# Moving a scratch write and refilling the router stage of a three-layer transformer kernel

## The reference

```python
for l in range(2):                       # hybrid_layer
    proj = x @ w_in[l]                   # gated delta rule (4 heads) + causal attention (8 heads)
    x = layer_norm(ALPHA * x + mix, ...)
    hid = causal_dwconv(x @ w_up, ffn_conv_w) + ffn_conv_b      # 2 x 2816 columns
    x = layer_norm(ALPHA * x + (silu(gate) * val) @ w_down, ...)
# second block
h = rms_norm(x, norm1_g)
# differential attention (4 heads) and dilated attention (8 heads), both with a bias by distance
x = x + concat([oa, od]) @ w_out
h = rms_norm(x, norm2_g)
aff = softmax(h @ w_router)              # 256 tokens x 16 experts
g, idx = top_k(aff.T, 32)                # each expert takes its 32 best tokens
ye = (silu(xe @ wg) * (xe @ wu)) @ wd * g   # xe = h[idx], 16 experts of 1024 x 2816
x = x + scatter_add(idx, ye)
out = rms_norm(x, norm_f_g)
```

## Time and profile before

| | us |
|---|---|
| median of 3 runs | 2328.2 |
| lowest and highest | 2315.79, 2331.55 |
| the profiled execution | 2328.16 |
| its span, first to last instruction | 2326.4 |

### The profile page before, as it was taken

The page is one execution under the profiler, slowest core; times in us unless marked ns, Lnnn a source line. Parts: engine busy times, 40 slices in busy tenths (PEclk is TensorE's granted clock), DMA queues, the critical chain, the costliest instruction groups (busy, mean ns, idle before and its releaser), DMA issues.

```text
span 2326.4 us, 29082 instructions
## 1 busy us (share of the span) xinstructions
PE 1814.8 (78%) x12246; PEld 975.5 (42%) x12246; DVE 469.3 (20%) x1096; ACT 307.6 (13%) x726; POOL 28.8 (1%) x38
## 2 busy tenths in 40 slices
PE   7899999999999999987666666655675666566565
PEld 6675886577488747642212212211221221122122
DVE  2334331253432213530101010100101010010011
ACT  2232221032311102420000000000000000000001
POOL 0010000001010000000000000000000000000000
PEclk9899999999999999987777777777767767676777
DMA  7543443432364346359999999999999999999998
GB/s 244 97 139 127 145 152 128 153 127 98 109 190 145 130 161 247 132 213 403 406 426 423 421 425 425 425 424 426 424 415 425 425 419 424 425 424 424 425 425 334
DMA packets 146422, 693.78 MB, mean 298 GB/s; under 512 B 12732, under 2 KB 62460, under 8 KB 92978
## 3 DMA queue, kind: packets, MB, share of 16 engines
q1 hardware_dynamic: 143346, 683.68, 73.2%
q0 software_dynamic: 2864, 9.00, 2.0%
q10 hardware_dynamic: 144, 0.13, 0.0%
HBM read 688.57 MB, written 4.19 MB: 298 GB/s over the span
## 4 chain that ended last, share of the span: by engine, by line
PE 49%; DMA 40%; SPq 4%; DVE 3%; issue 2%; DVEq 1%; ACT 1%; ACTq 0%
DMA arena<-in_w_up 30%; PE bank L565 16%; DMA arena<-in_w_down 9%; PE bank L588 6%; PE bank L691 6%; PE bank L1097 5%; PE bank L1114 3%; SPq L399 2%; SPq L407 1%; PE bank L890 1%; PE bank L686 1%; PE bank L976 1%; PE bank L914 1%; PE bank L972 1%; DVE arena L1853 1%
## 5 line engine op out<-in xcount | busy, mean ns | idle before, releaser
L1097 PE MATMUL bank<-arena 128*32 128x512 f32 (+1 forms) x3072 | 502.9, 811 | 311.1 <-DMA arena<-in_w_up 293.6
L1097 PEld LDWEIGHTS bank<-arena 128*32 128x32 f32 x3072 | 113.6, 144 | 696.7 <-DMA arena<-in_w_up 418.6
L565 PE MATMUL bank<-arena 128*128 128x256 f32 (+1 forms) x2208 | 383.1, 335 | 7.4 <-ACT arena L1142 3.4
L565 PEld LDWEIGHTS bank<-arena 128*128 128x128 f32 x2208 | 346.1, 192 | 46.4 <-ACT arena L1142 4.6
L1114 PE MATMUL bank<-arena 128*32 128x256 f32 x2816 | 237.5, 484 | 95.0 <-DMA arena<-in_w_down 94.9
L1853 DVE TENSOR_TENSOR arena<-arena,bank 64x256 f32<-64x256 f32 x96 | 40.1, 418 | 772.0 <-ACT arena L1376 770.3
L1114 PEld LDWEIGHTS bank<-arena 128*32 128x32 f32 x2816 | 94.9, 132 | 215.4 <-DMA arena<-in_w_down 132.7
L588 PE MATMUL bank<-arena 128*128 128x512 f32 x352 | 152.0, 591 | 0.0
L691 PE MATMUL bank<-arena 128*128 128x256 f32 x576 | 145.6, 401 | 0.0
L1376 ACT ACTIVATE arena<-bank 64x512 f32<-64x512 f32 (+1 forms) x48 | 23.2, 549 | 823.7 <-PE bank L1097 823.7
L691 PEld LDWEIGHTS bank<-arena 128*128 128x128 f32 x576 | 109.7, 198 | 20.8 <-issue 4.6
(11 more groups left out here) (277 smaller groups left out, 1166.2 us busy)
## 6 DMA issues: line engine op xcount, KB each, us to landing
arena<-in_w_gate SPq DMA_DIRECT2D x128, 1408.0 KB, 19.3
arena<-in_w_up SPq DMA_DIRECT2D x128, 1408.0 KB, 22.3
arena<-in_w_down SPq DMA_DIRECT2D x144, 1024.0 KB, 9.3
arena<-in_w_down SPq DMA_DIRECT2D x32, 1536.0 KB, 12.0
arena<-in_w_up SPq DMA_DIRECT2D x44, 1024.0 KB, 7.0
arena<-in_w_in SPq DMA_DIRECT2D x40, 1024.0 KB, 7.4
arena<-in_w_out SPq DMA_DIRECT2D x12, 1024.0 KB, 7.0
arena<-in_w_down SPq DMA_DIRECT2D x12, 512.0 KB, 3.3
```

The costliest lines, as they stand in the source:

```text
L565: last = mm(ps[bank][:, j * S + lo:j * S + lo + n], w[:, k, c:c + P], xT[:, k, lo:lo + n], start=(k == 0), stop=(k == KT - 1))
L1097: last = mm(ps[b][32 * q:32 * q + 32, 0:n], expert_x[:, k, :], weights[:, q // 2, c:c + n], start=(k == 0), stop=(k == KT - 1))
```

## The change

- The write of the bias rows is split into 12 writes, one a head, and goes behind layer 0's query rotation on GpSimd's queue; each waits for one more of layer 0's up products, from the fourth on. The read back waits for all twelve.
- SyncE: of the three down chunks ahead of gate_up(0, 2), two go behind it and its wait.
- PE: the first tile's logits move behind the second tile's rows; six of their eight k stand before the second tile's transposes, two behind. VectorE takes the first tile's `router_bias` between the second tile's copy of the transposes and its norm.
- PE: products of the identity with columns of `xT` into PSUM bank 0, whose result nobody reads (`keep_clock`): one of 512 columns behind the logits, four behind the transposes of the affinities, one of 256 columns behind each of the two later transposes.
- VectorE: the mask `taken` is signalled when it is made and is transposed by PE on its own, while the scan runs; the scan's numbers are transposed unmasked, and the multiplication by the mask is made on the transposed columns, in the place of the subtraction (the constants `slot` are 1 to 32 now, and 0 stands for "not taken").
- VectorE: the copy into `chosen_pair` comes behind the one-hot rows, with a semaphore of its own; the one-hot of each tile is signalled by itself, and PE begins with tile 0 at once.

```diff
@@ -101,7 +101,7 @@
     parts["causal"] = neg(jj <= i + P)
     parts["tok_row"] = np.broadcast_to(np.arange(S)[None, :], (P, S))
     parts["tok_col"] = np.concatenate([i, i + P], 1)
-    parts["slot"] = np.broadcast_to((np.arange(P) % CAP)[None, :], (P, P))
+    parts["slot"] = np.broadcast_to((np.arange(P) % CAP)[None, :] + 1, (P, P))
     at, cols = {}, 0
     for name, a in parts.items():
         at[name] = (cols, a.shape[1])
@@ -297,6 +297,7 @@
         lambda_parts = Region(second_attention.at + P + 256, after_experts_ring).take(8)
         router, rmax, rsum = second_tiny(T, NE + 1), second_tiny(T), second_tiny(T)
         slots, chosen_pair, places = second_tiny(T, NE + 1), second_tiny(T, 2), second_tiny(2)
+        taken_columns = second_tiny(T, NE)
         topv = second_tiny(8)[0:NE, :]
         routing = xT.rearrange("p x y -> p (x y)")[0:NE, 1280:2048].rearrange("p (x y) -> p x y", y=S)
         affT, affW, taken = (routing[:, i, :] for i in range(3))
@@ -419,10 +420,11 @@
             sp.wait_ge(sem("attended"), at(DEPTH, "attended", 8))
             gate_up(0, 1, 1)
             gate_up(0, 3, 3)
-            for k in range(3):
-                down(0, k)
+            down(0, 0)
             sp.wait_ge(sem("rows_used"), (DEPTH + 1) * ROW_UNITS + 2)
             gate_up(0, 2, 2)
+            for k in range(1, 3):
+                down(0, k)
 
             def stream_gate_up(e, ks):
                 for k in ks:
@@ -461,9 +463,6 @@
             pool.dma_start(const[:, 2 * P + 4:NC], a["consts"][:, 2 * P + 4:NC]).then_inc(sem("const_in"), 16)
 
 
-            pool.wait_ge(sem("bias_copied"), 1)
-            pool.wait_ge(sem("key_products"), 2)
-            pool.dma_start(scratch.rearrange("h (p n) -> h p n", p=P), distance_bias[0:BIAS_HEADS, :].unsqueeze(1).broadcast_to([BIAS_HEADS, P, 2 * S])).then_inc(sem("bias_out"), 16)
             for l in range(DEPTH):
 
                 pool.wait_ge(sem("q_shuffled"), at(l, "q_shuffled", 1))
@@ -472,11 +471,16 @@
                 nc.gpsimd.tensor_tensor(att_q, att_q, table("cos").unsqueeze(1).broadcast_to([P, 4, S]), ALU.mult)
                 pool.drain()
                 nc.gpsimd.tensor_tensor(att_q, att_q, q_swapped, ALU.add).then_inc(sem("q_rotated"), 1)
+                if l == 0:
+                    pool.wait_ge(sem("bias_copied"), 1)
+                    for h in range(BIAS_HEADS):
+                        pool.wait_ge(sem("up_product"), 4 + h)
+                        pool.dma_start(scratch[h:h + 1, :].rearrange("o (p n) -> o p n", p=P), distance_bias[h:h + 1, :].unsqueeze(1).broadcast_to([1, P, 2 * S])).then_inc(sem("bias_out"), 16)
 
 
             pool.wait_ge(sem("rows_used"), DEPTH * ROW_UNITS + 1)
             pool.dma_start(gain, a["norm1_g_2"].broadcast_to([P, D])).then_inc(sem("gain_in1"), 16)
-            pool.wait_ge(sem("bias_out"), 16)
+            pool.wait_ge(sem("bias_out"), 16 * BIAS_HEADS)
 
             def bias_of(h):
                 return scratch[h:h + 1, P - 1:P - 1 + P * (2 * S - 1)].rearrange("o (p n) -> (o p) n", p=P)[:, 0:3 * P]
@@ -1023,12 +1027,19 @@
                         last = tr(ps[H2_BANKS[2 * t + kh]][:, k * P:(k + 1) * P], x[:, t, (4 * kh + k) * P:(4 * kh + k + 1) * P], ident)
                     last.then_inc(sem("h2_transposed"), 1)
 
-            def logits(t):
-
-                pe.wait_ge(sem("h2_copied"), 2 * t + 2)
-                for k in range(KT):
+            def logits(t, ks):
+
+                if ks[0] == 0:
+                    pe.wait_ge(sem("h2_copied"), 2 * t + 2)
+                for k in ks:
                     last = mm(ps[2 + t][:, 0:NE], xT[:, k, t * P:(t + 1) * P], router_w[:, k, :], start=(k == 0), stop=(k == KT - 1))
-                last.then_inc(sem("logits"), 1)
+                if ks[-1] == KT - 1:
+                    last.then_inc(sem("logits"), 1)
+
+            def keep_clock(n, blocks=4):
+
+                for _ in range(n):
+                    mm(ps[0][:, 0:blocks * P], ident, xT[:, 0:blocks, 0:P], start=True, stop=True)
 
             unit_in(L, 7)
             for t in range(T):
@@ -1037,29 +1048,39 @@
                         pe.wait_ge(sem("attended_read"), at(L, "attended_read", k + 1))
                     elif k == 1:
                         rows_transposed(0)
-                    elif k == 3:
-                        logits(0)
                     for nh in range(2):
                         last = mm(ps[ROWS_BANKS[2 * t + nh]][:, :], mixT[:, 4 + k, t * P:(t + 1) * P], slot(7, 1024)[:, k, nh * 512:(nh + 1) * 512], start=(k == 0), stop=(k == 3))
                 last.then_inc(sem("rows_used" if t else "rows_t0"), 2 if t else 1)
+            logits(0, range(6))
             rows_transposed(1)
-            logits(1)
+            logits(0, range(6, KT))
+            logits(1, range(KT))
+            keep_clock(1)
             for t in range(T):
                 pe.wait_ge(sem("affinities"), t + 1)
                 tr(ps[6 + t][0:NE, t * P:(t + 1) * P], router[:, t, 0:NE], ident).then_inc(sem("affinities_transposed"), 1)
-
-            pe.wait_ge(sem("chosen"), 1)
-            for t in range(T):
-                last = tr(ps[7][:, NE * t:NE * t + NE], affW[:, t * P:(t + 1) * P], ident[0:NE, 0:NE])
-            last.then_inc(sem("slots_transposed"), 1)
+            keep_clock(4)
+
+            def token_columns(tokens, ready, bank, done):
+
+                pe.wait_ge(sem(ready), 1)
+                for t in range(T):
+                    last = tr(ps[bank][:, NE * t:NE * t + NE], tokens[:, t * P:(t + 1) * P], ident[0:NE, 0:NE])
+                last.then_inc(sem(done), 1)
+
+            token_columns(taken, "chosen", 5, "taken_transposed")
+            keep_clock(1, 2)
+            token_columns(affW, "counted", 7, "slots_transposed")
+            keep_clock(1, 2)
 
             def rows_gathered(done):
 
-                pe.wait_ge(sem("one_hot"), done)
                 for t in range(T):
+                    pe.wait_ge(sem("one_hot"), T * done - T + t + 1)
                     for q in range(4):
                         last = mm(ps[7][32 * q:32 * q + 32, 0:256], one_hot[:, t, 32 * q:32 * q + 32], normed_rows[:, t, 256 * q:256 * q + 256], start=(t == 0), stop=(t == T - 1))
                 last.then_inc(sem("rows_gathered"), 1)
+                pe.wait_ge(sem("pair_ready"), done)
                 for t in range(T):
                     last = mm(ps[2][:, 400:402], one_hot[:, t, :], chosen_pair[:, t, :], start=(t == 0), stop=(t == T - 1))
                 last.then_inc(sem("places_found"), 1)
@@ -1713,7 +1734,7 @@
 
             v.wait_ge(sem("second_small_in"), 112)
             w.tensor_mul(router_w, router_w, router_gain.unsqueeze(2).broadcast_to([P, KT, NE]))
-            w.memset(slots[:, :, NE:NE + 1], -1.0)
+            w.memset(slots[:, :, NE:NE + 1], 0.0)
             w.memset(router[:, :, NE:NE + 1], 0.0)
             w.tensor_copy(chosen_pair[:, :, 0], table("tok_col"))
             for n in range(2):
@@ -1772,6 +1793,8 @@
                 last.then_inc(sem("second_rows"), 1)
                 v.wait_ge(sem("h2_transposed"), 2 * t + 2)
                 w.tensor_copy(xT[:, 4:8, t * P:(t + 1) * P], ps[H2_BANKS[2 * t + 1]][:, :].rearrange("p (x y) -> p x y", y=P)).then_inc(sem("h2_copied"), 1)
+                if t == 1:
+                    router_bias(0)
                 rms(1, t, normed_rows, "h2_rows")
 
             def router_bias(t):
@@ -1789,7 +1812,6 @@
                 w.tensor_scalar(router[:, t, 0:NE], router[:, t, 0:NE], rsum[:, t:t + 1], None, ALU.mult).then_inc(sem("affinities"), 1)
 
             second_rows(0)
-            router_bias(0)
             second_rows(1)
             router_bias(1)
             affinities(0)
@@ -1806,21 +1828,20 @@
                 w.match_replace(nxt, topv, cur, -1.0)
                 v.drain()
             w.tensor_scalar(taken, affT, 0.0, None, ALU.is_lt)
+            v.drain().then_inc(sem("chosen"), 1)
+            w.tensor_tensor_scan(affW, taken, taken, 0.0, ALU.add, ALU.max)
+            v.drain().then_inc(sem("counted"), 1)
+            v.wait_ge(sem("taken_transposed"), 1)
+            w.tensor_copy(taken_columns, ps[5][:, 0:T * NE].rearrange("p (t n) -> p t n", n=NE))
             v.drain()
-            w.tensor_tensor_scan(affW, taken, taken, 0.0, ALU.add, ALU.max)
+            v.wait_ge(sem("slots_transposed"), 1)
+            w.tensor_mul(slots[:, :, 0:NE], ps[7][:, 0:T * NE].rearrange("p (t n) -> p t n", n=NE), taken_columns)
             v.drain()
-            w.tensor_mul(affW, affW, taken)
-            v.drain().then_inc(sem("chosen"), 1)
-            v.wait_ge(sem("slots_transposed"), 1)
-            w.tensor_scalar(slots[:, :, 0:NE], ps[7][:, 0:T * NE].rearrange("p (t n) -> p t n", n=NE), -1.0, None, ALU.add)
-            v.drain()
 
             def one_hot_rows(e):
 
-                w.tensor_copy(chosen_pair[:, :, 1:2], router[:, :, bass.ds(e, 1)])
                 for t in range(T):
```

(5 more changed lines are left out.)

## The result

The changed kernel takes 2342.55 us (median of 7 runs, 2338.99 to 2346.82), the kernel before 2328.2; ratio 1.0077, 95% interval 1.0053 to 1.0101. 2310 was forecast, a gain of 18; it became a loss of 14. The profiled execution has a span of 2344.8 us, 18.4 more than before.

| stretch | before | after | difference |
|---|---|---|---|
| to the 64-instruction run of layer 0 | 146.53 | 133.82 | -12.7 |
| layer 0's up products from the second tile on | 142.7 | 179.5 | +36.9 |
| from there to the router stage's row products | 631.7 | 629.1 | -2.6 |
| those to the third ring refill | 45.95 | 38.63 | -7.3 |
| to the end of the span | 1274.5 | 1278.6 | +4.2 |

The account below looks back on a forecast made before the run. PE's path before expert 0 was taken to set the start of the weight stream that paces the expert loop. Bias write -11.2 and router stage -7.0, others 0, gave -18.2: 2328.2 to 2310 us, range 2301 to 2322.

Parts of the forecast that it names:

- The hole (-11.2): Layer 0, PE idle near 95 us: bias write delays an instruction fetch; moving the write gains 11.2 us, bounds -11.2 and 0.
- The hole comes and goes: Lowest of three earlier runs, 2315.8, 12.4 under the median, read as a run whose instruction fetch was in time.
- The cost at the new place (0): Layer 0's up products: twelve writes of 3.8 us each leave w_up enough bandwidth; 0 taken, bounds 0 and 11.2 given back.
- 3.8 x 48 + 2.6 x 425: Up stage, each 6.4 us period: w_up gets 48 GB/s during a write, 425 after; 1.28 MB against 1.05 needed.
- the slower rival: Up stage: one-partition writes much slower, no gaps beyond 6.4 us each, PE stands 34 us; time 2344, chance 6%.
- Instructions at the new place: Up stage: PE takes instructions at a third of the old place's rate, so a late fetch has three times the slack.
- The router stage (-7.0): Router stage to expert 0: parts sum to 8.0 us, 1.0 taken off for the clock; bounds -8.2 and -1.5.
- the fill that no longer delays: Router stage: first tile's logits no longer precede the second tile's last quarter of rows, everything behind 1.7 us earlier.
- masks, copy and one-hot: Router stage behind top 32: mask multiplication leaves the path, pair's copy moves, PE begins on tile 0 early; -0.9 us.
- the clock: Identity products restore full clock from 0.50: gather to expert 0 gains 1.5 us, expert 0's first k 2.4.
- for which 1.0 was taken off: Router stage: clock falls, costing logits or transposes up to 1.5 us; four identity products may outlast top 32 by 1 or 2.
- SyncE's order, the loop (0): gate_up(0, 2) ahead of two down chunks costs 0; extra signals and later pair's copy in the expert loop hidden by stream.

Follow-up runs that it names:

- experiment 1: Changed kernel with the bias write put back as one DMA at its old place, router edits kept: 2321.54 us, ratio 0.9968.
- experiment 4: Changed kernel with one bias write at its old place, read from 96 partitions instead of twelve writes of one each: 2311.07 us, ratio 0.9935.
- 7: Changed kernel with the bias write as one unsplit DMA from 12 partitions behind up product 4: 2304.98 us, ratio 0.9916.
- experiment 3: Changed kernel with its twelve writes each taking ten or eleven copies of all twelve rows, from twelve partitions: 2307.08 us, ratio 0.9917.
- experiment 5: Experiment 3's kernel without its seven identity products (calls of `keep_clock` left out): 2312.55 us, ratio 0.9944.
- experiment 9: Changed kernel with its own twelve writes, same places and destinations, each read from eight partitions instead of one: 2306.69 us, ratio 0.9903.
- experiment 10: Changed kernel with its twelve one-partition writes scattered in HBM, copies of a row 24 KB apart: 2347.22 us, ratio 1.0084.

## Why the prediction was wrong, point by point

Both gains came: 12.7 and 7.3 us in the profile against 11.2 and 7.0. The miss is one term, the cost of the writes at their new place, which was put at 0 and measured 36.9.

- **The hole (-11.2).** Right: 54.73 us became 43.54. That the write is its cause is shown by experiments 1 (back with it), 4 and 7 (gone when the write is short, or stands elsewhere). That it is a late fetch of PE's instructions, the packets of q8 show. In the kernel before, the DMA queues from 84 to 101 us hold not one packet of the instruction queue q8; the next stretch, 101 to 102, does. The second line is the changed kernel's from 88 to 90 us, the third that of experiment 1 from 99 to 101 us:

```profile
q8 instruction: 1, 0.02, 5.8%
...
q8 instruction: 1, 0.02, 3.0%
...
q8 instruction: 1, 0.02, 2.9%
```

  By the packet records q8's packets start at 78.7, 88.7, 93.7 and 100.9 us in the changed kernel, at 80.2, 101.3, 104.9 and 113.6 in the kernel before, and at 78.8, 100.0, 103.7 and 112.3 in experiment 1. So the packet that should come 10 us after the first comes after 21, 11 us late, as much as the hole is worth. It was due near 90, some 4.6 us before PE stood still at 94.8, so it is not late because PE stood. PE starts again at 103.83. In experiment 4 it comes after 10.7 us, and there is no hole. No run took a fetch away by itself; what is left to argument is only that PE stood for want of that packet. The Trainium skill ("Runtime: NRT & Kernel Launch", Instruction fetch mechanics) gives PE room for 2048 instructions and calls the fetch mostly hidden; here the last packet before the hole lies in 80 to 84 us, and from 84 to 94.8 PE got through 184 recorded matmuls and 183 weight loads before it stood still, so the measurement is against that room (waits and register instructions are not in the count).
- **The hole comes and goes.** I read the lowest run of before as one without it. No profile caught such a run, so this is not shown. The times fit in part: experiment 1 keeps the old write and scatters from 2306.7 to 2327.5 us, experiment 3 lacks it and stays within 2304.6 to 2311.1, where the former's lowest runs lie. But the lowest run of the kernel before is 2306.8, some 20 us below its median, and the hole is worth 11.
- **The cost at the new place (0): the step that failed.** "A write of a twelfth should take 45.8 / 12 = 3.8 us" carried the duration of one DMA with twelve source partitions to twelve DMAs with one each. They run at a third of the rate per engine. Each then lasts beyond the 6.9 us between two up products, the writes overlap without a gap, and the sum "3.8 x 48 + 2.6 x 425" has no second term: w_up gets 66 GB/s, against the 48 that I used for a load beside a write. That is 0.46 MB a period where the sum had 1.28 and PE needs 1.05, and PE stops for 34.3 us. The mechanism of the slower rival (no gap beyond 6.4 us, PE out of w_up) is what happened; what was wrong was its 6%. That its 34 us and its 2344 came out so nearly is in part luck: it had writes of 10 us and 120 us of them with w_up at 48 GB/s, where the eleven writes ahead of PE's restart took 98 us, 8.9 each, and w_up got 7.81 MB in the 103 us from the first issue to that restart, 76 GB/s. The 6% rested on "the old write also read one row at a time, if its packets leave in order", a guess that no row of the trace showed; by the packet records the old write has up to twelve packets under way, the number of its rows, and the twelve new ones up to sixteen, on one row. A bound from both sides (3.8 us if the rate is the engines', 45.8 if it is the partition's) would have covered it, and the range with it.
- **Instructions at the new place.** Right: no hole without a releaser opens in the up stage with any of the writes. A fetch is late there too: the q8 packet behind the one near 242 us starts at 284.3 in the changed kernel and at 269.4 in experiment 3. As forecast, instructions are used up so slowly there (27 us from packet to packet in experiment 3) that PE was still busy until w_up ran out.
- **The router stage (-7.0).** Right: -7.3 in the profile, -6.2 by the medians of experiment 1. Inside it: the fill that no longer delays gave its 1.7; the logits their 1.3 (1.97 us at a granted clock of 1.00, not the first tile's 1.69); the transposes ahead of them nothing of their 0.2 (1.11 us as before); masks, copy and one-hot 0.7 of the 0.9; the clock 1.4 of 1.5 from the gather to expert 0, and 2.1 of 2.4 in expert 0's first three k. Two identity products of 0.63 us, costed at 0, stand on the chain between the masks' transposes and the gather; without them, at half clock, that stretch is as long (2.31 us in experiment 5, 2.26 in 3). Neither thing came for which 1.0 was taken off: the logits ran ahead of the clock's fall, and top 32 did not wait for the four identity products (4.53 us from the affinities' transpose to the mask, 4.52 before). There are seven identity products, not six. The clock fell where I expected it and the four in a row brought it back under top 32; without them it costs 4.1 us (experiment 5). The Trainium skill's rule that transposes do not count as busy time ("TensorE: Matmul & The Clock Gate", Part 4) is neither borne out nor refuted: no run had transposes alone ahead of a fall. What the prediction drew from it, a fall during the logits, did not come: they ran at 1.00, and in the changed kernel and in experiment 1 the clock fell while the identity product behind them ran (0.60 in 1048 to 1049; 0.72 in 1024 to 1026), in experiment 5, which has none, behind the logits (they end at 1011.65; 0.66 in 1012 to 1014).
- **SyncE's order, the loop (0).** Right: expert 0 never waits for its k = 2, and the loop's length does not follow the edits.

## What to carry to other kernels

The time of this DMA did not divide by its bytes: what it was divided along decided. A write that repeats a row from one SBUF partition should be spread over more source partitions first (in experiment 9 the matmul that makes the row replicated it, at no cost that the time shows). If it is split, each part should take copies of all rows and not all copies of one. And a cost of 0 that is owed to "there is room beside it" needs the rate of the thing that moves in, taken from a row with the same shape, or a bound from the worst one.

## What the runs showed of the hardware that I had not expected

- The rate of a broadcast write, as bytes over engine time, GpSimd's queue: from one partition 2.2 GB/s per engine (changed kernel); eight 8.7 (experiment 9); twelve 11.1 as twelve writes (3) and 6.8 to 7.1 as one DMA (before, 7); 96 18.2 (4). The number of partitions is not the whole of it. The twelve short writes and the one long one have the same packet of 0.61 us when eleven or twelve are under way; the short ones are faster on the mean because they spend much of their time with fewer, at 0.16 us each.
- In the table under experiment 10, sixteen engines on one partition draw 30 GB/s together, less than eight engines on eight partitions.
- Slow packets do not only take their own time: the engines count as 0.92 busy at 58 GB/s, and everything that shares them waits, loads of weights (18 to 75 us instead of 5 to 9) and instruction packets (15 us in the up stage, 11 in the hole of the kernel before). The waiting is between the packets: a packet of SyncE's queue takes 0.186 x 16 x 56 us / 3653 = 46 ns beside the slow writes and 0.461 x 16 x 56 us / 8489 = 49 ns in experiment 3.
- Seven matmuls with the identity, whose result nobody reads, are worth 4.1 us in a stage of latencies (experiment 5), through the clock of what follows.
